# Convolution groups 1 and 2 of each hybrid layer: from four weight-stationary tiles to a token-stationary unit with two turned halves

## What is computed

```
def conv_mixer(h, b_gate, c_gate, conv_w):
    u = c_gate * h
    y = lax.conv_general_dilated(u, conv_w[:, None, :], window_strides=(1,),
                                 padding=((CONV_WIDTH - 1, 0),), ...
                                 feature_group_count=D_CONV)
    return b_gate * y
...
    proj = x @ w_in
    (q_lat, kv_lat, k_rope, g_mla, p_in, g_pool, c_h, c_b, c_c, g_conv) = jnp.split(proj, split_idx, axis=-1)
...
    y_conv = conv_mixer(c_h, c_b, c_c, conv_w) * jax.nn.silu(g_conv)
    mix = jnp.concatenate([y_mla, y_pool, y_conv], axis=-1)
    out = mix @ w_out + b_out
```

## Time and profile before

| | us |
|---|---|
| median of 3 runs | 2535.31 |
| lowest and highest | 2535.24, 2536.07 |
| the profiled execution's own time | 2535.32 |
| its span in the trace | 2533.5 |
| PE busy | 2513.5 (99%) |
| DVE busy | 1848.1 (73%) |
| ACT busy | 1315.6 (52%) |
| HBM traffic, mean over the span | 189 GB/s |

### The profile page before, as it was taken

The page is one execution under the profiler, slowest core; times in us unless marked ns, Lnnn a source line. Parts: engine busy times, 40 slices in busy tenths (PEclk is TensorE's granted clock), DMA queues, the critical chain, the costliest instruction groups (busy, mean ns, idle before and its releaser), DMA issues.

```text
span 2533.5 us, 33176 instructions
## 1 busy us (share of the span) xinstructions
PE 2513.5 (99%) x12124; PEld 2111.2 (83%) x12124; DVE 1848.1 (73%) x2980; ACT 1315.6 (52%) x1893; POOL 17.5 (1%) x20
## 2 busy tenths in 40 slices
PE   7999999999999999999999999999999999999999
PEld 6888888888888888888888887888888888888888
DVE  8787658777658777677777785678777767777766
ACT  6665565565566444444444555775544444444443
POOL 2000000000000000000000000000000000000000
PEclk9999999999999999999999999999999999999999
DMA  8555556454555555555555554444555555555554
GB/s 302 198 186 180 190 192 232 169 188 174 196 186 186 196 195 189 195 185 200 198 191 183 186 204 150 150 152 174 191 199 186 195 184 198 200 194 189 197 183 150
DMA packets 71519, 480.84 MB, mean 190 GB/s; under 512 B 8032, under 2 KB 10720, under 8 KB 18144
## 3 DMA queue, kind: packets, MB, share of 16 engines
q1 hardware_dynamic: 71392, 479.16, 54.0%
HBM read 475.72 MB, written 2.10 MB: 189 GB/s over the span
## 4 chain that ended last, share of the span: by engine, by line
PE 83%; DVE 1%; ACT 1%; issue 0%; ACTq 0%; DVEq 0%
PE acc L937 13%; PE acc L939 13%; PE acc L938 12%; PE score L937 9%; PE score L939 9%; PE score L938 9%; PE acc L923 9%; PE acc L927 4%; PE score L923 1%; PE score L1263 1%; PE score L927 1%; PE head_ps L1286 0%; DVE low L1740 0%; PE turn_ps L1272 0%; PE head_ps L1287 0%; PE sums L1206 0%
## 5 line engine op out<-in xcount | busy, mean ns | idle before, releaser
L1740 DVE TENSOR_TENSOR low<-raw,high 128x1024 fp32r<-128x1024 f32 (+3 forms) x916 | 1080.2, 1184 | 472.8 <-ACT high L1338 464.5
L1338 ACT ACTIVATE high<-raw 128x1024 fp32r<-128x1024 f32 (+3 forms) x916 | 935.5, 1024 | 844.6 <-PE acc L939 443.4
L923 PE MATMUL acc<-xs,high 128*128 128x512 f32 x1184 | 396.2, 397 | 2.4 <-DVE xs L2275 2.2
L937 PE MATMUL acc<-high,xs 128*128 128x512 f32 x960 | 379.4, 395 | 0.4 <-DVE scale_a L1833 0.3
L939 PE MATMUL acc<-low,xs 128*128 128x512 f32 x960 | 374.1, 390 | 0.0
L938 PE MATMUL acc<-high,xs 128*128 128x512 f32 x960 | 373.7, 389 | 0.0
L927 PE MATMUL acc<-xs,low 128*128 128x256 f32 x1184 | 297.9, 279 | 0.0
L937 PE MATMUL score<-high,xs 128*128 128x512 f32 x704 | 274.0, 389 | 0.0
L939 PE MATMUL score<-low,xs 128*128 128x512 f32 x704 | 273.9, 389 | 0.0
L938 PE MATMUL score<-high,xs 128*128 128x512 f32 x704 | 273.9, 389 | 0.0
L923 PEld LDWEIGHTS acc<-xs,high 128*128 128x128 f32 x1184 | 219.4, 188 | 50.5 <-DVE xs L2275 3.1
(11 more groups left out here) (399 smaller groups left out, 3222.3 us busy)
## 6 DMA issues: line engine op xcount, KB each, us to landing
raw<-w_up_dram SPq DMA_DIRECT2D x176, 1024.0 KB, 4.8
raw<-w_in_dram SPq DMA_DIRECT2D x76, 1024.0 KB, 4.9
raw<-w_wide_dram SPq DMA_DIRECT2D x70, 1024.0 KB, 4.8
raw<-w_out_dram SPq DMA_DIRECT2D x32, 1024.0 KB, 4.8
raw<-w_heads_dram SPq DMA_DIRECT2D x24, 1024.0 KB, 4.8
raw<-w_mixout_dram SPq DMA_DIRECT2D x16, 1024.0 KB, 4.8
raw<-w_down_dram SPq DMA_DIRECT2D x16, 704.0 KB, 4.1
raw<-w_mem_dram SPq DMA_DIRECT2D x8, 1024.0 KB, 4.8
```

The source lines that it names most:

```text
L923: return eng.matmul(bank_, hi, moving, start=start, stop=False)
L937: eng.matmul(bank_, xh, hi, start=start, stop=False)
L1338: eng.activation(high[:, s % SPLIT, to:to + n * P], raw[:, s % RAW, at_:at_ + n * P], ACT.Copy).then_inc((highs_a, highs_b)[piece], 1)
L1740: eng.tensor_tensor(low[:, s % SPLIT, w], raw[:, s % RAW, at_:at_ + n * P], high[:, s % SPLIT, w].bitcast(F32), ALU.subtract).then_inc((lo ...
```

## The change

Tiles 1 to 8 of `in_d` (groups 1 and 2) become a region `conv` of eight slabs, slots 35 to 42. A unit is one group: four slabs of `_rows` layout, 512 weight columns (gc, c_h, c_c, c_b) by 2048 rows, multiplied by `product_natural`, as six matmuls of 512 columns for each of 16 row blocks. Its two halves of the tokens lie in an `acc` and in `sums` for unit 1, in both `acc` for unit 2. ACT copies each half to `conv_nat` (`conv_copies`) and applies silu to its gate columns (`conv_gate`). DVE makes two products with the tokens on the partitions, c_h x c_c and silu(gc) x c_b, into `conv_prod`, and turns both into `branch[:, 2:4]` with 16 transposes of 32-row strips, eight in each of two slots (`conv_move`). Then `conv` applies the taps and multiplies. The last group stays in four tiles, region `in_e`, slots 43 to 46, with its first tile in `sums`. `conv_gate` of group 1 is in slot 39 (before: silu in slot 37), `conv` in slot 41 (before 38); of group 2 in slots 43 and 45 (before: 41 and 42). `out` begins at number 47, so nothing in it moves. As many slabs are loaded and split as before.

```diff
--- before.py
+++ after.py
+CONV_UNITS = 2
...
-            Region(f"in_d{layer}", 13, (8, 8), 13, 2),
+            Region(f"in_d{layer}", 1, (8, 8), 1, 2), Region(f"conv{layer}", 4 * CONV_UNITS, (8, 8), 0, 2),
+            Region(f"in_e{layer}", 4, (8, 8), 4, 2),
...
-        put(33 + 4 * g, "silu", layer, 12 + g, 13 + g)
-        put(34 + 4 * g, "conv", layer, g)
+        if 1 <= g <= CONV_UNITS:
+            put(35 + 4 * g, "conv_gate", layer, g)
+            put(35 + 4 * g, "conv_move", layer, g, 0)
+            put(36 + 4 * g, "conv_move", layer, g, 1)
+            put(37 + 4 * g, "conv", layer, g)
+        else:
+            put(33 + 4 * g, "silu", layer, 12 + g, 13 + g)
+            put(34 + 4 * g, "conv", layer, g)
...
-    put(48 + 4, "shift", ln)
-    put(48 + 5, "moments", ln, 0)
-    put(48 + 8, "moments", ln, 1)
-    put(48 + 12, "moments", ln, 2)
+    put(47 + 4, "shift", ln)
...
-    TURNED_OVER |= {(f"in_d{_l}", k) for k in (1, 3, 5, 7, 9, 11)}
+    TURNED_OVER |= {(f"in_e{_l}", 2)}
...
+        conv_nat = at("conv_nat", [P, TB, 2 * S], F32, cursor[0] - 4 * S * MEM)
...
+        conv_prod = at("conv_prod", [P, TB, S], F32, cursor[0])
...
+            if r.conv:
+                a, c = (acc[(r.t0 + n) % 2][:, :] for n in range(2))
+                return ((a, sums[:, :]), (c, a))[k // r.span][b]
...
+            if r.name[:4] == "in_e" and T == r.t0:
+                return sums[:, :]
...
+                    elif r.name[:4] == "in_e" and tile < 3:
+
+                        eng.wait_ge(conv_out, 2 * REG[f"conv{r.layer}"].conv0 + 2 + tile)
...
-                                last = product_natural(unit_bank(r, k, b), (xs if r.up else hidden)[:, row, :],
+                                last = product_natural(unit_bank(r, k, b), (hidden if r.wide else xs)[:, row, :],
...
+                            if r.conv and q_ == 0 and piece == 0:
+                                conv_bank_free(r, u, b)
                             for c in range(per):
+                                if r.conv and 4 * piece + 2 * b + c == (middle + 1) // 2:
+                                    for step in halfway:
+                                        do(*step)
...
+            def conv_bank_free(r, u, b):
+
+                if u == 0:
+                    eng.wait_ge(stored, REG[f"in_d{r.layer}"].t0)
+                elif u == 1 and b == 0:
+                    eng.wait_ge(stored, REG[f"in_d{r.layer}"].t0 + 1)
+                else:
+                    eng.wait_ge(conv_out, 2 * r.conv0 + 1)
...
+            def conv_copies(r, k, i):
+
+                n = r.conv0 + k // r.span
+                if n:
+                    eng.wait_ge(conv_gated, n)
+                for b in range(TB):
+                    if b == 0:
+                        eng.wait_ge(unit_half, halves_till(r, k, i))
+                    else:
+                        eng.wait_ge(products, r.g0 + 2 * (k + r.span))
+                    eng.activation(conv_nat[:, b, :], unit_bank(r, k, b), ACT.Copy).then_inc(conv_out, 1)
...
+                elif kind == "conv_gate":
+                    n = REG[f"conv{a[0]}"].conv0 + a[1]
+                    eng.wait_ge(conv_out, 2 * n)
+                    eng.activation(conv_nat[:, :, 0:P], conv_nat[:, :, 0:P], ACT.Silu).then_inc(conv_silu, 1)
...
+                elif kind == "conv_gate":
+                    layer, g = a
+                    n = REG[f"conv{layer}"].conv0 + g
+                    eng.wait_ge(conv_silu, n)
+                    eng.tensor_tensor(conv_prod[:, :, P:S], conv_nat[:, :, P:2 * P], conv_nat[:, :, 2 * P:3 * P], ALU.mult)
+                    eng.tensor_tensor(conv_prod[:, :, 0:P], conv_nat[:, :, 0:P], conv_nat[:, :, 3 * P:4 * P], ALU.mult)\
+                        .then_inc(conv_gated, 1)
+                    eng.wait_ge(conv_gated, n)
+                elif kind == "conv_move":
+                    layer, g, half = a
+                    from_ = conv_prod[:, :, :].rearrange("p b (m j f) -> p j b m f", m=2, f=QUAD)
+                    to = branch[:, 2:4, :].rearrange("p m (b q s) -> p q b m s", b=TB, s=QUAD)
+                    for n in (2 * half, 2 * half + 1):
+                        for j in range(P // QUAD):
+                            ins = eng.transpose(to[QUAD * j:QUAD * (j + 1), n, :, :, :], from_[QUAD * n:QUAD * (n + 1), j, :, :, :])
+                    if half:
+                        ins.then_inc(conv_turned, 1)
                 elif kind == "conv":
                     layer, g = a
 
                     def tap(w):
                         return p_("conv", (3 * layer + w) * GROUPS + g)
 
-                    eng.wait_ge(stored, conv_tile(layer, 4 * g + 2) + 1)
-                    u, y = silu_g[:, :], scale_c[:, 0:S]
-                    step_(eng.tensor_tensor(u, branch[:, 0, :], branch[:, 1, :], ALU.mult))
+                    y = scale_c[:, 0:S]
+                    if 1 <= g <= CONV_UNITS:
+                        eng.wait_ge(conv_turned, REG[f"conv{layer}"].conv0 + g)
+                        u = branch[:, 3, :]
+                    else:
+                        eng.wait_ge(stored, conv_tile(layer, 4 * g + 2) + 1)
+                        u = silu_g[:, :]
+                        step_(eng.tensor_tensor(u, branch[:, 0, :], branch[:, 1, :], ALU.mult))
                     step_(eng.tensor_scalar(y, u, tap(2), None, ALU.mult))
                     for back in (1, 2):
                         step_(eng.scalar_tensor_tensor(out=y[:, back:S], in0=u[:, 0:S - back], scalar=tap(2 - back),
                                                        in1=y[:, back:S], op0=ALU.mult, op1=ALU.add))
 
-                    eng.wait_ge(gated, gates_done(layer, 12 + g))
-                    step_(eng.tensor_tensor(mix[:, 12 + g, :], mix[:, 12 + g, :], y, ALU.mult))
+                    if 1 <= g <= CONV_UNITS:
+                        step_(eng.tensor_tensor(mix[:, 12 + g, :], branch[:, 2, :], y, ALU.mult))
+                    else:
+                        eng.wait_ge(gated, gates_done(layer, 12 + g))
+                        step_(eng.tensor_tensor(mix[:, 12 + g, :], mix[:, 12 + g, :], y, ALU.mult))
...
-    out["w_in"] = np.concatenate([_tiles(a["w_in"][l], columns) for l in range(DEPTH)])
+    to = len(columns) - 512 * (GROUPS - 1 - CONV_UNITS)
+    from_ = to - 512 * CONV_UNITS
+    out["w_in"] = np.concatenate([w for l in range(DEPTH) for w in (
+        _tiles(a["w_in"][l], columns[:from_]), _rows(a["w_in"][l][:, columns[from_:to]], 4, 512),
+        _tiles(a["w_in"][l], columns[to:]))])
```

More of the change, by code:

```diff
@@ L114, in plan @@
         r.per = 2 if r.name[:3] == "mem" else 4
-        r.kind = next((k for n, k in (("up", "unit"), ("wide", "unit"), ("down", "down"), ("uq", "uq"), ("uk", "uk"), ("uv", "uv"),
+        r.kind = next((k for n, k in (("up", "unit"), ("wide", "unit"), ("conv", "unit"), ("down", "down"), ("uq", "uq"), ("uk", "uk"), ("uv", "uv"),
                                       ("pool", "pool"), ("mem", "natural"), ("nat", "natural"), ("heads", "natural"),
@@ L124, in plan @@
                    "down2": "w_down2"}[
-                       next(n for n in ("in_", "uq", "uk", "uv", "pool", "out", "mem", "nat", "heads",
+                       next(n for n in ("in_", "conv", "uq", "uk", "uv", "pool", "out", "mem", "nat", "heads",
                                         "mixout", "up1", "up2", "wide1", "wide2", "down1", "down2") if r.name.startswith(n))]
@@ L132, in plan @@
             r.loop = (4, 8, 4)
[L133 to L136, removed]
+        r.span = WIDE if r.wide else 4
+        r.unit0, r.up0, r.wide0, r.conv0 = units, ups, wides, convs
+        ups, wides, convs = (n + kind * r.n // r.span for n, kind in ((ups, r.up), (wides, r.wide), (convs, r.conv)))
+        units = ups + wides + convs
         if r.name in ("up10", "up20"):
@@ L228, in put @@
         for name, first in (("in_a", 0), ("uq", 16), ("uk", 20), ("uv", 21), ("in_b", 23), ("in_c", 31),
-                            ("pool", 33), ("in_d", 34), ("out", 48)):
+                            ("pool", 33), ("in_d", 34), ("conv", 35), ("in_e", 43), ("out", 47)):
             r = REG[f"{name}{layer}"]
@@ L815, in conv_tile @@
                 return REG[f"in_a{layer}"].t0 + 15
-            return REG[f"in_c{layer}"].t0 + n - 1 if n < 3 else REG[f"in_d{layer}"].t0 + n - 3
+            if n < 3:
+                return REG[f"in_c{layer}"].t0 + n - 1
+            return REG[f"in_d{layer}"].t0 if n == 3 else REG[f"in_e{layer}"].t0 + n - 4 * GROUPS + 4
         def after_norm(r):
@@ L946, in middle_of @@
                     return 8 + k // 2
-                if r.name[:4] == "in_d":
-                    return (8, 9, 10, 11, 11 + 2 * r.layer, 12 + 2 * r.layer, 8)[k // 2]
+                if r.conv:
+                    return (8, 9, 10, 11, 11 + 2 * r.layer)[(k + 1) // 2]
+                if r.name[:4] == "in_e":
+                    return (11 + 2 * r.layer, 12 + 2 * r.layer, 12 + 2 * r.layer, 8)[k]
                 return 8
```

(10 more changed lines are left out.)

22 lines of the change are left out of this document (13 added, 9 removed).

## The result

| | before | after |
|---|---|---|
| median, us | 2535.27 (8 runs) | 2542.8 (8 runs) |
| lowest and highest | 2535.18, 2536.07 | 2541.49, 2544.38 |
| ratio after/before, 95% interval | | 1.0029 [1.0019, 1.0038] |
| the profiled execution's own time, span | 2535.32, 2533.5 | 2544.07, 2542.3 |
| granted clock over the span | 1.00 | 0.998 |

The changed kernel is **7.5 us slower**: the side is that of the forecast, but the time lies above its range, which ended at 2541.2. Its runs also spread over 2.9 us, where those of before spread over 0.9.

What follows compares the result with a forecast made beforehand. PE's unbroken chain of matmuls was taken to bound the kernel. 2535.3 - 1.7 (shorter stream) + 5.6 (waits at `out`) = 2539.2 us, taken as 2539.0, range 2533.5 to 2541.2: no change that counts, on the slow side.

Steps and rivals of the forecast that it cites:

- Part 1: PE's matmul stream: slabs at 5.44 us replace tiles at 5.54 to 5.59; -1.7 us over both layers.
- slow starts: PE's matmuls after each of some five interruptions per layer: 0.05 us allowed for each, 0.25 us a layer.
- Parts 2 and 3: Banks and first unit, and DVE and ACT in slots 35 to 42: no added wait of PE, nothing.
- margins of 0.2 and 0.9: Last head's gating in slot 44: DVE caught up by 0.2 us (layer 0) and 0.9 us (layer 1).
- rival B: Group 2's first half ends late in slot 43, delaying the gating and PE: 2541.1 us, chance 0.16.
- Part 4: DVE's queue ahead of `out`, slots 44 to 46: late store makes PE wait 2.5 and 3.1 us, +5.6 us.
- Together +5.6 us: PE's waits for the last `in_e` store at `out`, 2.5 us in layer 0 plus 3.1 in layer 1.
- It can't be made up: After PE's one wait per layer at `out`: PE is full afterwards, so the lost time stays lost.
- upper bound, 7.7: DVE queue ahead of `out`: the wait term rises to 7.7 us if ACT's waits stay despite late DVE.
- Rival A: DVE's queue ahead of `out` isn't late, so only the shorter PE stream counts: 2533.6 us, chance 0.14.
- rival C: PE's pace doesn't improve with the slabs, so no stream gain: 2540.9 us, or 2540.5; chance 0.06.

Runs made afterwards that it cites:

- E3: Changed kernel with group 2's four tap instructions (1.89 us of DVE) moved behind the last store of `in_e`; 2535.96 us, 1.0003.
- E5: Changed kernel without seven of the eight transposes of group 2's second half, 2.2 us of DVE's queue; 2535.56 us, 1.0000.
- E1: Changed kernel with the second half of `out`'s first unit in the free bank `sums`, DVE's work unchanged; 2534.31 us, 0.9997.
- E2: Changed kernel with 11 (layer 0) and 14 (layer 1) useless matmuls into `sums` ahead of PE's wait; 2539.73 us, 1.0018.
- E6: Kernel before with 3 (layer 0) and 4 (layer 1) useless DVE additions ahead of the last store of `in_d`; 2538.27 us, 1.0011.
- E4: Kernel before with 6 (layer 0) and 8 (layer 1) useless DVE additions ahead of the last store of `in_d`; 2544.72 us, 1.0036.
- E7: Kernel before with 5 useless DVE additions in each layer ahead of the last store of `in_d`; 2541.61 us, 1.0023.
- E8: Kernel before with the second half of `out`'s first unit put in the bank `sums`, as a control; 2535.36 us, 1.0000.

## Why the prediction was right in its mechanism and wrong in its price

**Part 1, -1.7 us: right in total.** -0.75 and -0.94 us up to `out`, with 5.44 us for a slab. Within it, two errors offset each other. The eight slabs of `conv` took 50.89 us in each layer where the tiles took 51.81 (213.54 to 265.35 in layer 0; slot 43 starts there, and not at 264.8, where rows 6 are cut), so they gained 0.92 and not 0.75: the slow starts were counted too high. The four tiles of `in_e` gained nothing (-0.17 and +0.02 us) where 0.10 was counted. The rule of the Trainium skill (TensorE: Matmul & The Clock Gate, Back-to-back issue gap) that is weighed there, by which only 0.4 us would come, does not hold for these shapes: 0.2267 us where it has 0.216, and 1.8 us gained in the `conv` slots.

**Parts 2 and 3, nothing: right.** PE has no wait in slots 35 to 46, and DVE waited 0.73 and 0.56 us for PE ahead of the last gating, where margins of 0.2 and 0.9 were counted. So the chain of rival B did not happen. Its outcome did, slower by more than 0.2%, for a reason that it does not have.

**Part 4: the mechanism and the waits right, the price wrong.** The store came 2.90 and 3.62 us later where 2.86 and 3.42 were forecast, PE waited 2.43 and 3.17 us where it was 2.5 and 3.1, and E3, E5 and E1 took the wait away by the queue and by the bank. The step that failed is "**Together +5.6 us**": the wait was priced by its length alone. "It can't be made up" was as far as it went, and that TensorE comes back from such a stop at a lower clock was nowhere in it. By E2 the clock costs 3.0 us more at the median (4.2 in the profiled execution).

A smaller part was missing too, and it shows in every run with a stop. PE is 0.17 us later than the idle time in brackets says, and the first step behind a stop takes 0.34 us instead of 0.23, at full clock too. That is 0.28 us a stop. With it the sums of the kernels whose clock stayed up come out within 0.3 us:

| kernel | sum: its before, -1.7 for the changed stream, idle, 0.28 a stop | measured, us |
|---|---|---|
| E1 | 2535.2 - 1.7 + 0.3 + 0.3 = 2534.1 | 2534.31 |
| E2 | 2535.2 - 1.7 + 5.6 + 0.6 = 2539.7 | 2539.73 |
| E3 | 2535.2 - 1.7 + 1.8 + 0.6 = 2535.9 | 2535.96 |
| E5 | 2535.6 - 1.7 + 1.1 + 0.6 = 2535.6 | 2535.56 |
| E6 | 2535.6 + 2.4 + 0.6 = 2538.6 | 2538.27 |

(E2's stop is filled; its 5.6 is that of the changed kernel.) So the term of Part 4 is 5.6 + 0.6 + 3.0 = 9.2 us and not 5.6. Even its upper bound, 7.7, was a bound on the wait alone. With 9.2 the sum is 2535.3 - 1.7 + 9.2 = 2542.8, as measured. That also moves the case from within 0.2% to slower.

The trace of before had a row that could have led there. Behind its one long wait, 13.4 us at the start, the same eight matmuls take nearly twice as long as ten microseconds later:

```profile
15.12 1.91 PE L1314 MATMUL head_ps<-par,z 128*128 128x128 f32 x8
...
25.20 1.03 PE L1314 MATMUL head_ps<-par,z 128*128 128x128 f32 x8
```

It was put down to the start. The granted clock printed for that stretch is 1.00, but that stands for no record: the trace's first clock record begins at 17.1 us, and in the trace of after at 21.5 us. There the pace changes too: matmuls of 512 columns, each with one of 256 behind it, start 0.64 us apart at 20.38 and 21.02 in the kernel after, and 0.35 apart at 21.61 and 21.96. That the clock is the cause at the start is argued from this, and no experiment shows it. The kernel before has no wait between that one and 1 us, so its rows could not say at what length the price begins; they could have warned that there is one.

**Rival A** (no wait) and **rival C** (no better pace) did not happen; A's number, 2533.6, is what E1 reaches within 0.7 us once the wait is gone. **The version to keep** is E1: 2534.31 against 2535.23 before on its chip, 0.9 us, which the measurement can't tell from nothing, and some 8.4 us less than the change as it was made, each against its own chip's before.

## What to carry to other kernels

Before a step is moved into the queue ahead of a store, look for the margin at which another engine would take that store's buffer, though no list of waits shows it; here it was 0.3 us, and of 4.4 us of added work 2.9 and 3.6 us reached the store. On a TensorE that is otherwise always busy, price a stop with the slower matmuls behind it as well, here from 1.87 us on and half as much again as the idle time. The remedy can be another free buffer and not less work: here one of eight PSUM banks stood idle.

## What the runs showed of the hardware

- TensorE's granted clock went from 2.4 to 1.2 GHz around stops of 2.32 us and more in both executions that were traced (after, E4), and in 7 of 10 runs of the kernel with stops of 1.87 us (E7). It never did in the traced executions with stops of 0.20 to 1.41 us (E3, E5, E6), and the other runs of those kernels print 1.00 as well. The slow pace lasted for 3 to 6 us of nearly unbroken matmuls.
- The fall need not meet the stop. In layer 1 of the kernel after it came about 1 us before the stop ended, in layer 0 of E4 it came 1 us after PE had taken up its work again.
- At full clock too a stop costs 0.28 us more than the idle time printed for it (E3: 0.53 printed, 0.70 us late, and 0.33 us for the first step instead of 0.23).
- A kernel with stops that lower the clock also scatters: 2.9 us from lowest to highest (after, 8 runs), 4.2 (E4, 6 runs), 3.5 (E7, 10 runs), against 0.7 to 1.2 in E1, E2, E3, E5, E6 and E8 (10 or 11 runs each) and 0.9 to 1.5 in the kernel before (8 to 31 runs). Such a spread, with a mean granted clock of 0.998 or 0.999, points to the clock before any timeline is opened.
- A DVE queue that is never idle passes on what is taken out of it or put into it to within 0.1 us: 1.89 us out shortened the waits by 1.9 (E3), 2.2 out by 2.2 (E5), and each useless addition of 0.45 us put in just ahead of the store lengthened them by 0.46 (E6, E7, E4: 0.95, 1.87 and 2.32 us in layer 0 with 3, 5 and 6 of them).
